# One 2 MB transfer in place of two 1 MB transfers in an expert-weight stream, with the contraction order permuted

## The reference, cut to what matters

```python
logits = h @ w_router + b_router                  # h: 512 x 1024
top_val, top_idx = lax.top_k(logits, 4); gates = softmax(top_val)
# for each expert e, on the tokens that chose it:
gu   = xb @ w_gate_up[e] + b_gate_up[e]           # 1024 x 2048, 8 MB in float32
act  = (clip(gu[:, 1024:], -7, 7) + 1) * gate * sigmoid(1.702 * gate)   # gate = min(gu[:, :1024], 7)
yb   = act @ w_down[e] + b_down[e]                # 1024 x 1024, 4 MB in float32
out += gates * yb
```

## Time and profile before

| | |
|---|---|
| time, median of 3 runs | 1305.59 us (1304.23 to 1307.17) |
| the profiled execution's own time | 1307.32 us |
| its span (first to last instruction) | 1305.6 us |
| TensorE matmul busy | 1259.9 us, 97% |
| TensorE weight load busy | 747.6 us, 57% |
| VectorE / ScalarE / GpSimd busy | 521.2 / 189.9 / 162.6 us |
| bytes moved | 455.73 MB, mean 349 GB/s |
| weight loads of the experts | 384 of 1 MB, median 10.0 us (gate/up) and 9.9 us (down) from issue to landing |

### The profile page before, as it was taken

The page is one execution under the profiler, slowest core; times in us unless marked ns, Lnnn a source line. Parts: engine busy times, 40 slices in busy tenths (PEclk is TensorE's granted clock), DMA queues, the critical chain, the costliest instruction groups (busy, mean ns, idle before and its releaser), DMA issues.

```text
span 1305.6 us, 52682 instructions
## 1 busy us (share of the span) xinstructions
PE 1259.9 (97%) x21821; PEld 747.6 (57%) x21821; DVE 521.2 (40%) x1733; ACT 189.9 (15%) x437; POOL 162.6 (12%) x267
## 2 busy tenths in 40 slices
PE   7999999999999999999999999999999999988885
PEld 4446654545666665665665665666656656644552
DVE  6454223447333333343343343333433433422337
ACT  3431123332001000000000000010000000000002
POOL 4100330122101101101011011011011010000111
PEclk9999999999999999999999999999999999999998
DMA  6453131619999999999999999999999999999997
GB/s 224 147 193 131 34 130 49 258 65 342 404 421 407 421 410 422 417 420 410 419 416 421 412 422 414 422 417 420 413 416 421 416 421 417 420 421 421 421 425 283
DMA packets 80504, 455.73 MB, mean 349 GB/s; under 512 B 11057, under 2 KB 23018, under 8 KB 30730
## 3 DMA queue, kind: packets, MB, share of 16 engines
q1 hardware_dynamic: 76400, 445.69, 83.8%
q0 software_dynamic: 3888, 8.40, 1.7%
q10 hardware_dynamic: 106, 0.04, 0.0%
HBM read 432.53 MB, written 23.27 MB: 349 GB/s over the span
## 4 chain that ended last, share of the span: by engine, by line
PE 52%; DMA 44%; DVE 2%; issue 1%; SPq 0%; ACT 0%; POOL 0%; POOLq 0%; ACTq 0%; DVEq 0%
DMA ring<-in_w_gate_up_dram 26%; PE ps L1924 18%; DMA ring<-in_w_down_dram 16%; PE ps L1492 11%; PE ps L1976 8%; PE ps L1512 4%; PE ps L1890 3%; PE ps L1553 2%; DMA x_rows_dram<-cat,rowi 1%; PE ps L1916 1%; PE ps L1546 1%; PE ps L1967 0%; DMA ring<-in_x_dram 0%; DMA ring<-x_rows_dram 0%; PE ps L1899 0%
## 5 line engine op out<-in xcount | busy, mean ns | idle before, releaser
L1924 PE MATMUL ps<-ring,cat 128*32 128x256 f32 x9856 | 550.1, 380 | 7.6 <-DMA ring<-in_w_gate_up_dram 7.6
L1924 PEld LDWEIGHTS ps<-ring,cat 128*32 128x32 f32 x9856 | 306.6, 110 | 219.9 <-DMA ring<-in_w_gate_up_dram 10.9
L1976 PE MATMUL ps<-ring,cat 128*32 128x256 f32 x4800 | 276.2, 380 | 13.2 <-DMA ring<-in_w_down_dram 12.6
L1976 PEld LDWEIGHTS ps<-ring,cat 128*32 128x32 f32 x4800 | 142.6, 110 | 118.1 <-DMA ring<-in_w_down_dram 11.3
L1492 PE MATMUL ps<-hbuf,ring 128*128 128x512 f32 x320 | 147.7, 608 | 1.7 <-DVE hbuf L922 1.7
L1313 DVE TENSOR_REDUCE wslot<-ps 128x2 f32<-128x6 f32 x75 | 12.4, 165 | 318.7 <-ACT cat L848 317.1
L606 POOL DMA_INDIRECT pair_rows_dram<-cat,rowi x73 | 72.7, 996 | 432.1 <-ACT cat L848 432.1
L840 ACT ACTIVATE cat<-cat 128x128 f32<-128x128 f32 x154 | 47.7, 309 | 516.8 <-DVE cat L1337 516.8
L1890 PE MATMUL ps<-hbuf,cat 128*32 128x256 bf16 x2432 | 105.2, 273 | 0.6 <-DVE cat L1410 0.6
L1492 PEld LDWEIGHTS ps<-hbuf,ring 128*128 128x128 f32 x320 | 58.9, 192 | 68.2 <-issue 65.8
L1337 DVE TENSOR_SCALAR cat<-ps 128x128 f32<-128x128 f32 x154 | 44.8, 291 | 128.8 <-PE ps L1924 128.7
(11 more groups left out here) (369 smaller groups left out, 818.5 us busy)
## 6 DMA issues: line engine op xcount, KB each, us to landing
ring<-in_w_gate_up_dram SPq DMA_DIRECT2D x256, 1024.0 KB, 10.0
ring<-in_w_down_dram SPq DMA_DIRECT2D x128, 1024.0 KB, 9.9
ring<-in_w_in_dram SPq DMA_DIRECT2D x10, 1024.0 KB, 6.3
pair_rows_dram<-cat SPq DMA_DIRECT2D x4, 2048.0 KB, 10.9
ring<-pair_rows_dram SPq DMA_DIRECT2D x4, 2048.0 KB, 20.6
ring<-in_w_out_dram SPq DMA_DIRECT2D x1, 4096.0 KB, 12.9
ring<-in_x_dram SPq DMA_DIRECT2D x4, 512.0 KB, 5.4
x_rows_dram<-ring SPq DMA_DIRECT2D x2, 1024.0 KB, 9.7
```

The costliest lines, as they stand in the source:

```text
L1924: last = mm(ps[SLOTS * q:SLOTS * (q + 1), banks[half], 0:2 * P].rearrange("p (s m r) -> p s m r", s=2, m=2), x[:, SLOTS * u:SLOTS * (u + 1 ...
L1976: last = mm(ps[SLOTS * q:SLOTS * (q + 1), 1, 0:QD], actT[:, c // 4, SLOTS * (c % 4):SLOTS * (c % 4 + 1)], w[:, i, q * QD:(q + 1) * QD], st ...
```

## The change

Two neighbouring units (2k, 2k+1) of one expert come as one transfer of 2 MB in place of two. For that their content changes: the pair of `w_gate_up` units covers 256 rows, of which a partition gets two neighbouring ones, the pair of `w_down` units covers 512 rows, four neighbouring ones to a partition. A partition's share of a pair is then 16 KB without a break in HBM. A unit is one half of that, 8 KB to a partition, at a distance of 16 KB.

`doubled(n)` says which pairs are joined: n even and 32 <= n < 372. These are 170 transfers in place of 340. Units 20 to 31 and the last expert's 12 stay single, as do the first 20. `refill` skips the odd unit of a joined pair, and waits at the even one until TensorE has used up both old units (`used + u + units`) and until the transfer that brings unit n - 4 has landed. `arrival(n)` gives the semaphore and count of the transfer that brings unit n: for an odd unit of a pair that is the even slot's. TensorE's `landed` waits for it too.

The order of the contraction follows the new content: the gather's moving side takes every second element, the first matmul's columns are chosen in longer pieces, and VectorE reads PSUM with a step of four elements.

```diff
         def quarter(v, q, half):
-            pairs = v.rearrange("p s (m r) -> p s m r", r=2 * P)
-            return pairs[:, :, 2 * half:2 * half + 2, 2 * SLOTS * q:2 * SLOTS * (q + 1)]
+            fours = v.rearrange("p s (m r) -> p s m r", r=4 * P)
+            return fours[:, :, half, P * q:P * (q + 1)]
         def in_order(v):
-            return v.rearrange("p (m i c) -> p m c i", m=2, c=2)
+            return v.rearrange("p (i c) -> p c i", c=4)
         def chunked_half(v):
-            return v.rearrange("p (m c i) -> p m c i", m=2, c=2)
+            return v.rearrange("p (c i) -> p c i", c=4)
...
-        def unit_src(e, u):
+        def unit_src(e, u, units=1):
             if u < NGU:
-                return w_gate_up[0, bass.ds(e, 1), u * P:(u + 1) * P, :].rearrange("a p c -> (a p) c")
-            r = 2 * P * (u - NGU)
-            return w_down[0, bass.ds(e, 1), r:r + 2 * P, :].rearrange("a (p c) n -> (a p) (c n)", c=2)
+                r = 2 * P * (u // 2)
+                rows = w_gate_up[0, bass.ds(e, 1), r:r + 2 * P, :].rearrange("a (p c) n -> (a p) (c n)", c=2)
+            else:
+                r = 4 * P * ((u - NGU) // 2)
+                rows = w_down[0, bass.ds(e, 1), r:r + 4 * P, :].rearrange("a (p c) n -> (a p) (c n)", c=4)
+            return rows[:, u % 2 * UNIT:(u % 2 + units) * UNIT]
...
+        def doubled(n):
+            return RING + NU <= n < NU * (E - 1) and n % 2 == 0
+        def arrival(n):
+            lead = n - 1 if n % 2 and doubled(n - 1) else n
+            loads = [k for k in range(lead % RING, lead + 1, RING) if not (k % 2 and doubled(k - 1))]
+            return slot_in[lead % RING], 16 * len(loads)
...
-                    if n >= NU * E:
+                    if n >= NU * E or n % 2 and doubled(n - 1):
                         continue
-                    landed = n - AHEAD
-                    sp.wait_ge(w_used, used + (u + 1))
+                    units = 2 if doubled(n) else 1
+                    signal, count = arrival(n - AHEAD)
+                    sp.wait_ge(w_used, used + (u + units))
                     if e == 0 and u >= NGU:
                         sp.wait_ge(side_ps, 2 + u + 1 - NGU)
-                    sp.wait_ge(slot_in[landed % RING], (landed // RING + 1) * 16)
-                    load_unit(following[n // NU - e], n % NU, n % RING)
+                    sp.wait_ge(signal, count)
+                    load_unit(following[n // NU - e], n % NU, n % RING, units)
...
-                            rows = h2p[n][:, b, :].rearrange("p (j r) -> p j r", r=P)[:, :, SLOTS * q:SLOTS * (q + 1)]
-                            last = mm(ps[SLOTS * q:SLOTS * (q + 1), 2, 0:QD].rearrange("p (j i) -> p j i", i=SLOTS),
+                            rows = h2p[n][:, b, :].rearrange("p (m r c) -> p m c r", r=P, c=2)[:, :, :, SLOTS * q:SLOTS * (q + 1)]
+                            last = mm(ps[SLOTS * q:SLOTS * (q + 1), 2, 0:QD].rearrange("p (m c i) -> p m c i", c=2, i=SLOTS),
                                       hot[:, b, 0, :], rows, start=b == 0 and n == 0, stop=b == blocks - 1 and n == 2)
...
-                slot, turn = slot_of(e, u)
-                pe.wait_ge(slot_in[slot], (turn + 1) * 16)
+                slot, _ = slot_of(e, u)
+                pe.wait_ge(*arrival(NU * e + u))
...
-                        "p (s m r) -> p s m r", s=2, m=2), x[:, SLOTS * u:SLOTS * (u + 1)],
+                        "p (s r) -> p s r", s=2), x[:, SLOTS * u:SLOTS * (u + 1)],
                         quarter(w, q, half), start=opens and u == 0, stop=u == NGU - 1)
```

More of the change, by code:

```diff
@@ L310, in chain, with unit_dst @@
             return link
-        def unit_src(e, u):
+        def unit_src(e, u, units=1):
             if u < NGU:
-                return w_gate_up[0, bass.ds(e, 1), u * P:(u + 1) * P, :].rearrange("a p c -> (a p) c")
-            r = 2 * P * (u - NGU)
-            return w_down[0, bass.ds(e, 1), r:r + 2 * P, :].rearrange("a (p c) n -> (a p) (c n)", c=2)
-        def unit_dst(slot, u):
-            return ring[:, slot * UNIT:(slot + 1) * UNIT]
+                r = 2 * P * (u // 2)
[4 more added lines that the diff above has]
+            return rows[:, u % 2 * UNIT:(u % 2 + units) * UNIT]
+        def unit_dst(slot, units=1):
+            return ring[:, slot * UNIT:(slot + units) * UNIT]
+        def doubled(n):
[4 more added lines that the diff above has]
+            return slot_in[lead % RING], 16 * len(loads)
         def slot_of(j, u):
@@ L378, in _, with load_unit @@
             sp.dma_start(wrt[:, :, :], w_router[0].rearrange("(k p) e -> p k e", p=P)).then_inc(pool_router_in, 16)
-            def load_unit(e, u, slot):
-                sp.dma_start(unit_dst(slot, u), unit_src(e, u)).then_inc(slot_in[slot], 16)
+            def load_unit(e, u, slot, units=1):
+                sp.dma_start(unit_dst(slot, units), unit_src(e, u, units)).then_inc(slot_in[slot], 16)
             load_unit(0, 0, 0)
@@ L1916, in gate_up_bias @@
                         last = mm(ps[SLOTS * q:SLOTS * (q + 1), banks[half], 0:2 * P].rearrange(
-                            "p (s m r) -> p s m r", s=2, m=2), selu[:, :], quarter(bias, q, half), start=start, stop=False)
+                            "p (s r) -> p s r", s=2), selu[:, :], quarter(bias, q, half), start=start, stop=False)
                 last.then_inc(gub_used, 1)
```

## The result

| | before | after |
|---|---|---|
| median | 1306.38 us, 4 runs (1304.23 to 1307.63) | 1325.78 us, 4 runs (1323.45 to 1332.43) |
| ratio | | 1.0161, 95% interval 1.0127 to 1.0195 |

The change makes the kernel slower by 19 us by the medians and 21 us by the ratio. Forecast were 1300.3 us, 5 us faster, with a range that ran to 1311.

A forecast was written before the change was run, and what follows sets the result against it. TensorE was taken to bound phase A narrowly, with DMA as full, and DMA alone phase B. Waits 2.0 + earlier first pair 1.7 + cheaper pairs 1.6 = 5.3 us off 1305.6 gives 1300.3 us, range 1295 to 1311.

The forecast's parts named there:

- rhythm: Repeat of 24 units in SP's weight loads, 61.65 us; five TensorE blocks, as experts alternate between two and three.
- phase A: Stretch from 353 to 1156 us, TensorE and DMA both full; TensorE the bound by 0.1 to 0.2 us in 61.5.
- Packets: Weight loads: 16 KB runs cost 1.3% less a byte than 8 KB runs, 0.065 us off a pair's 4.98 us.
- Phase B: Stretch from 1156 to 1267 us, DMA alone sets the pace: 30.7 us for an expert's weights against 24.6 us.
- From unit 320 on: Loads from the last full ring: first pair lands 1.7 us earlier, then 25 pairs at 0.065 save 1.6 us.
- Depth: When a pair lands, one pair (4.9 us) is still under way, cover enough against a 2.2 us start; nothing.
- Both units of a pair: Last pair of an odd expert lands 43.3 us after the pause's end, TensorE wants it at 44.2; 0.9 us early.
- Phase A's 2.0 us of waits: Of TensorE's 3.2 us of waits for weights in phase A, 2 us go (bounds 0 and 3.2).
- SP, columns, VectorE: Half the issues on SP, first matmul's longer column pieces, VectorE's PSUM reads with a step of four: each nothing.
- The gather: L1890 in each block: strided moving side taken at 0, bounds 0 and 1.31 us; rival that it slows TensorE, chance 0.11.
- The scatter: Rival: a block's scatter round trip becomes the bound above 9.4 us; plain scatter put at 8.6; chance 0.06.
- The 16 KB rival: Weight loads: 16 KB transfers stream slower, 5.1 us for a pair, 20 us in all, 1322 to 1326 us; chance 0.03.

The follow-up runs named there:

- e1_singles: The changed kernel with every transfer single (1 MB, 8 KB runs 16 KB apart in HBM), permuted contraction order kept: 1306.9 us, ratio 1.0013.

## Why the prediction was wrong, by its own steps

*What bounds the kernel, and the rhythm.* Right: phase A has two resources full within 0.2 us in 61.5, and in after the time is decided by one pair in each rhythm. It was right too that this pair is the last of an odd expert, and "TensorE waiting once in every rhythm" was named as a sign of being wrong.

*Packets.* Right at depth 6, not at the depth of the change. Forecast were 0.065 us a pair. Phase B gave 0.066 for the longer runs alone. Joined pairs with both kinds of runs at depth 6 and a contiguous gather differ by 1319.1 - 1310.3 = 8.8 us over 170 pairs, 0.052 us each. The row of 8 us and the row of 5 us gave the right size. In after itself a megabyte cost 38.8 engine-us in phase A, more than before.

*From unit 320 on.* The rate was right, as just said. The head start of 1.7 us was smaller. In after the stream wasn't idle when unit 320 was issued: the pair before it landed 1.9 us later, at 1117.96, and the new pair came 7.5 us after its issue, where 7.1 were forecast. Against unit 321 of before, 9.6 us behind its pause's end, and with the 0.86 us for the second slot, that is 1.2 us. At depth 6 it is 0.1 us (9.1 in before, 8.1 in after). It no longer mattered, since unit 320 itself came 17.6 us later.

*Depth.* The step that failed first. The prediction had one pair of 4.9 us still under way when a pair lands, called that cover enough against a start of 2.2 us, and put it at nothing. The runs show 16 us: that is what a third pair under way gives back in after (1325.8 to 1309.8); it is 12 us with pairs of 8 KB runs and 11 us with 1 MB transfers issued in pairs. The sum treated the 16 engines as one. A transfer signals its slot 16 times, and in after these signals of one pair are spread over 2.0 us (median) and up to 3.6. Less the 0.2 us from landing to issue and the start of 2.2, the pair still under way covers a spread of 2.5 us; by this estimate the cover fails at every fifth pair (27 of 137), for the part of the engines that is ahead. What is lost there isn't made up, since phase A has no slack. That these engines stood idle is argued, as the packets don't name their engine; the fall of the queue's share from 98.1% to 96.3% fits it.

*Both units of a pair.* The second step that failed, by its size. The sum put the critical pair at 43.3 us, 42.4 of them from the first issue behind the pause, against 44.2 at which TensorE wants it. It came 43.7 after that issue, even with three pairs under way. The first landing of the row took 8.0 us and not 7.1, and the other seven 0.4 us more together. These 0.4 were in the prediction's own rows: 38.0 engine-us a MB are 4.98 us for a pair of 2.097 MB, and it took 4.92. With the 0.86 us of the second slot on top it is 44.6: 0.9 us to spare became 0.4 us late, once in every rhythm: 62.24 against 61.73 us, 6 us over 12 rhythms, of which phase B gives 2.3 back. That is about the 4.0 us between 1309.8 and 1305.8. At depth 4 the two steps meet in this pair: it came 44.8 us (mean) after that issue. A margin of 0.9 us out of a sum of 43 was no margin; the forecast should have counted what each further 0.5 us costs (6 us over 12 rhythms).

*Phase A's 2.0 us of waits.* They were to go, and on the matmuls' own row they grew from 0.7 to 11.4 us (the 3.2 us of the earlier trace rows are on the weight loads' row).

*SP, columns, VectorE.* Right at nothing: the first matmul takes 380 ns and VectorE's read of PSUM 291 ns, as before.

*The gather.* Taken at 0, measured at 0.06 us a block (4.6% of 1.31). With single loads it is at most the 1.7 us of `e1_singles`; in after it hides behind the late pair. The 0.08 us from which this rival was to decide wasn't reached. The Trainium skill ("SBUF — State Buffer", Door 1) has reads with two or more hits in a line of 16 bytes at full rate. The trace is within 5% of that, but not at it.

*The scatter.* It lands in 6.8 us (median), 9.0 at most in phase A of after, below the 9.4 from which it would have been the bound. That rival was rightly small.

*The slower side.* No rival had the mechanism that came. The 16 KB rival named a time near the measured one (1322 to 1326), for a reason that the runs exclude. The Trainium skill ("SBUF — State Buffer", The DMA setup-cost knee) says, in short, to coalesce into the largest single transfer, because each has a fixed cost of some 2 us. In this case's stretch the queue holds more than one transfer outside the pauses, and the row shows 417 GB/s with 1 MB transfers, so there was no such cost to save. Apart from the longer runs, larger transfers only made the grain of everything that waits for them coarser.

So the account of the 20 us, each a difference between two measured kernels at depth 4: the time of issue (two free slots, a whole pair landed) +15; the joined transfer +11; the longer runs and the layout -5. The first two are uncertain by some 6 us each, as the kernel between them varies, and the third by as much as itself. At depth 6 the same differences are +4, +10 and -9; there the second was shown to be TensorE's wait for both halves. How the first divides between the wait for two slots and the wait for a whole pair was not told apart in a run of its own, but 11 of the 15 us go with more depth.

## What to carry to other kernels

Joining two transfers into one does three things at once: it doubles the grain in which the stream is topped up, it makes the consumer wait for the second half, and it changes the runs. Here, where the queue is kept full, only the last was a gain, 1 to 2% of the DMA time. Count the depth in transfers left when SP is released, not in bytes, and where it must be joined, add depth at the same time (here 16 of 20 us). And in a kernel with two full resources, find the one transfer of a rhythm that arrives last and write down its margin, and what each microsecond beyond it costs: a small stall there is paid in each rhythm, while a cost elsewhere (the gather's) may be paid nowhere.

## What the runs showed of the hardware

- Depth for 8 KB packets in one queue: four units of 1 MB keep 16 engines at 38.5 engine-us a MB, three don't (38.8, and 8.6 us in this kernel), and six give nothing more. For 2 MB pairs two under way are too few (38.8, 96.3% busy), three give 38.0, and four no more.
- With less under way more packets are long: 833 of 18328 over 1.2 times the median with two pairs under way, 306 of 18645 with three; of 8 KB packets 617 of 37314 with three units, 271 of 37584 with four. The cause is open.
- A run of 16 KB is one packet of 611 ns (median); two of 8 KB are 622. Between the pauses the stream reaches 425 to 430 GB/s with them and 420 to 422 with 8 KB. The rate over 353:1156 in 40 equal slices, after with the permutation stored and depth 6, then the kernel that differs from before in the time of issue and in both halves:

```profile
GB/s 411 423 429 379 427 425 389 426 430 393 425 428 390 426 427 393 430 427 401 426 429 401 413 427 419 386 427 430 379 430 427 389 424 428 377 429 426 383 429 426
```

```profile
GB/s 401 423 421 384 420 420 397 421 420 396 422 420 390 422 420 379 419 422 416 386 421 421 390 422 420 395 422 421 393 420 420 393 421 421 392 423 420 388 422 422
```

  About every third slice has the pause of a rhythm: in both the ring is full there, and DMA loses some 2 us of a slice of 20 us (389 of 427 GB/s), although TensorE will wait for a pair some 44 us later.
- ScalarE's copy of 128 x 512 from float32 to bf16 takes 630 ns with contiguous writes, 685 ns with a step of 8 bytes in the reads, and 2636 ns when neighbours are written 256 bytes apart. Which of the short inner loop and the scattered writes does it wasn't told apart.
- A bf16 moving side with a step of two elements costs a gather of four column groups 4 to 5%, with the single matmul's time in the profile unchanged (271 to 272 ns against 273).
